# Forty tile transposes of a decoder-block kernel moved from TensorE to DMA on SyncE's queue

## The reference

```
h   = rms_norm(x, norm_mix)
b_a, c_a, u_a, u_p, q_x, g_a, g_p, g_x = split(h @ w_in)                  # 8 x 1024 columns
y_a = (b_a * causal_dwconv3(c_a * u_a)) @ w_conv_out
y_p = per-group linear map of (trailing mean over 2/4/8/16 - token) * pool_scale
y_x = softmax(q_x k^T / 16) v @ w_xattn_out                                # k, v from rms_norm(mem), 256 tokens, 4 heads
x   = x + (sigmoid(g_a)*y_a + sigmoid(g_p)*y_p + sigmoid(g_x)*y_x) @ w_out
h   = rms_norm(x, norm_ffn)
x   = x + (silu(h @ w_gate) * (h @ w_up)) @ w_down                         # 2816 wide
out = rms_norm(x, norm_final)
```

## Time and profile before

| | |
|---|---|
| median of three runs | 1171.29 us |
| the profiled execution | 1170.21 us |
| its span on the slowest core (core 3) | 1168.6 us (all cores 1164.9 to 1168.6) |
| granted TensorE clock, mean | 0.996 to 0.997 |
| TensorE matmul busy | 1137.1 us (97%) |
| VectorE busy | 477.6 us (41%) |
| ScalarE busy | 330.6 us (28%) |
| chain that ended last | PE 91%, DVE 3%, ACT 2%, issue 2%, DMA 1% |
| DMA queue of GpSimd (weights), of SyncE | 39.4%, 14.7% of 16 engines' span |

### The profile page before, as it was taken

One profiled execution on the slowest core, in us unless ns is written; L12 is line 12 of the kernel. 1 busy time (PEld: TensorE's weight loads), 2 busy tenths in 40 slices (PEclk: granted clock), 3 DMA queues, 4 the chain that ended last, 5 costly groups with the idle time before them and its releaser, 6 DMA issues.

```text
span 1168.6 us, 15156 instructions; the slowest of 8 cores (1164.9 to 1168.6 us)
## 1 busy us (share of the span) xinstructions
PE 1137.1 (97%) x5852; PEld 557.7 (48%) x5852; DVE 477.6 (41%) x480; ACT 330.6 (28%) x512; POOL 74.3 (6%) x144
## 2 busy tenths in 40 slices
PE   4899989999999999999999999999999999999997
PEld 2566555454554444444444444444444444444443
DVE  4533555465656654553454632111324221112222
ACT  5333444425222434442121210111524121111111
POOL 1101000101001010001001000200000000000000
PEclk9899999999999999999999999999999999999999
DMA  9999830367296758125226452999954254200132
GB/s 238 174 185 208 140 70 21 80 143 132 62 189 160 223 117 186 38 45 109 49 61 108 64 153 108 177 194 168 191 122 159 90 111 82 43 1 1 36 117 100
DMA packets 35382, 135.89 MB, mean 116 GB/s; under 512 B 4187, under 2 KB 4187, under 8 KB 34800
## 3 DMA queue, kind: packets, MB, share of 16 engines
q0 software_dynamic: 20160, 77.64, 39.4%
q1 hardware_dynamic: 15008, 57.03, 14.7%
q10 hardware_dynamic: 144, 0.26, 0.1%
HBM read 185.27 MB, written 23.07 MB: 178 GB/s over the span
## 4 chain that ended last, share of the span: by engine, by line
PE 91%; DVE 3%; ACT 2%; issue 2%; DMA 1%; DVEq 0%; ACTq 0%; SPq 0%; another core or an unknown queue 0%; POOLq 0%
PE ps L228 89%; PE ps L341 2%; DVE tmp L378 1%; DMA ring<-w_in 1%; ACT tmp L402 1%; DVE tmp L371 1%; ACT tmp L375 0%; DMA arena<-x 0%; DVE smx L399 0%; ACT hb L317 0%; DVE hb L329 0%; DVE arena L383 0%; DVE hA L345 0%; ACT L402 0%; DVE ring L542 0%
## 5 line engine op out<-in xcount | busy, mean ns | idle before, releaser
L228 PE MATMUL ps<-hA,ring 128*128 128x512 bf16 (+1 forms) x2496 | 511.6, 365 | 13.2 <-DVE stat L325 4.5
L228 PEld LDWEIGHTS ps<-hA,ring 128*128 128x128 bf16 x2496 | 244.2, 98 | 271.6 <-issue 16.2
L228 PE MATMUL ps<-arena,ring 128*128 128x512 bf16 (+1 forms) x1600 | 331.4, 366 | 0.1
L228 PEld LDWEIGHTS ps<-arena,ring 128*128 128x128 bf16 x1600 | 156.0, 98 | 167.9 <-issue 0.8
L228 PE MATMUL ps<-arena 128*128 128x512 bf16 x832 | 182.2, 379 | 0.0
L612 DVE TENSOR_TENSOR arena<-ps,tmp 128x1024 bf16<-128x1024 f32 x44 | 53.9, 1224 | 228.5 <-PE ps L228 220.4
L228 PEld LDWEIGHTS ps<-arena 128*128 128x128 bf16 x832 | 80.9, 98 | 95.3
L608 ACT ACTIVATE tmp<-ps 128x1024 f32<-128x1024 f32 x44 | 45.1, 1024 | 253.8 <-PE ps L228 253.8
L453 DVE TENSOR_TENSOR tmp<-tmp 128x1024 f32<-128x1024 f32 (+6 forms) x40 | 49.2, 1230 | 43.0 <-ACT tmp L443 40.5
L228 PE MATMUL ps<-ring,arena 128*128 128x512 bf16 x256 | 57.9, 379 | 0.0
L218 POOL DMA_DIRECT2D ring<-w_in x48 | 25.6, 539 | 445.0 <-PE ps L228 264.3
(11 more groups left out here) (83 smaller groups left out, 614.9 us busy)
## 6 DMA issues: line engine op xcount, KB each, us to landing
ring<-w_in POOLq DMA_DIRECT2D x48, 512.0 KB, 13.7
ring<-w_gate_up POOLq DMA_DIRECT2D x44, 512.0 KB, 14.4
arena<-x SPq DMA_DIRECT2D x32, 512.0 KB, 10.0
tmp<-x_scr SPq DMA_DIRECT2D x24, 512.0 KB, 6.1
x_scr<-arena SPq DMA_DIRECT2D x16, 512.0 KB, 2.9
out<-tmp SPq DMA_DIRECT2D x15, 512.0 KB, 2.9
arena<-w_down POOLq DMA_DIRECT2D x2, 2816.0 KB, 50.1
ring<-w_kv POOLq DMA_DIRECT2D x8, 512.0 KB, 18.4
```

The costliest lines, as they stand in the source:

```text
L228: ins = e.matmul(o, l, r, start=s0, stop=s1)
```

## The change: forty calls of `transpose` become `dma_transpose`

A new helper issues one DMA transpose on SyncE's queue from the `hb` buffer straight to the transposed tile in SBUF. No TensorE instruction, no PSUM bank and no copy remain of these tiles. Two pieces of order change too: the softmax tile's transpose is issued at once after the tile is normalized (the delay of up to two tiles is gone), and `b_trans` follows each `b_fin` at position 1 of a merge chunk instead of position 2.

```diff
+    def dma_transpose(b, dst, dkeys):
+        src = hbt(b)
+        plan.op("sp", lambda e: e.dma_start_transpose(out=dst, in_=src[:, :]), reads=[b.key()], writes=dkeys, dma=True)
...
     def score_t(hf, hbi, i):
-        transpose(hbi, V_PT[hf][0][:, :, i * P:(i + 1) * P], V_PT[hf][1])
+        dma_transpose(hbi, V_PT[hf][0][:, :, i * P:(i + 1) * P], V_PT[hf][1])
...
     def c_trans(b, i, on_dve=False):
-        transpose(b, HA[:, :, TOK0 + i * P:TOK0 + (i + 1) * P], [("HA", i + 1)], on_dve=on_dve)
+        dma_transpose(b, HA[:, :, TOK0 + i * P:TOK0 + (i + 1) * P], [("HA", i + 1)])
...
     def b_trans(i):
-        transpose(b_c[i][0], HB[:, :, i * P:(i + 1) * P], kA(A_H, 8), on_dve=(i % 2 == 0))
+        dma_transpose(b_c[i][0], HB[:, :, i * P:(i + 1) * P], kA(A_H, 8))
...
                 b_fin(i)
+                b_trans(i)
                 b_fin(i + 1)
-        if pos == 2 and j in (2, 3, 5, 6):
-            i = {2: 0, 3: 2, 5: 4, 6: 6}[j]
-            b_trans(i)
-            b_trans(i + 1)
+                b_trans(i + 1)
+        if pos == 2:
             if j == 6:
...
     def s_step(H, i):
-        if len(s_pend) > 1:
-            score_t(*s_pend.pop(0))
-        s_pend.append((H.hf, score(H, i).finish(), i))
+        score_t(H.hf, score(H, i).finish(), i)
```

## The result

The changed kernel takes 1156.19 us (median of five runs; 1155.57 to 1157.67 but for one of 1272.15). The kernel before took 1170.97 us in the same five rounds. The ratio is 0.9873 with a 95% interval of 0.9861 to 0.9886: 14.8 us faster, where the forecast of 1153.5 us meant 17.5 us; the range of 1150 to 1166 holds the time.

A forecast was written before the change was run, and what follows sets the result against it. TensorE, busy 97% of the span, was taken as the bound. 17.8 - 0.45 + 0.57 - 0.5 = 17.4 us off 1170.2 gave 1152.8, on the median's scale 1153.9; forecast 1153.5 us, range 1150 to 1157, about 0.8 for 1150 to 1166.

The forecast's parts named there:

- The block price, 0.445 us, and 40 of them: Each tile's eight transposes cost TensorE 0.445 us; removing 40 such blocks in five stages gains 17.8 us.
- -0.45 and -0.5 in half 0's score stage: One removed block there only lengthens a wait for ScalarE's copy (0.45 us); 0.5 us more kept as a small loss.
- +0.57 for waits for a tile to be transposed: TensorE's waits of 0.40 us at 379.70 and 0.17 us at 428.05 would go too.
- A block that goes is a block gained: Four of five stages have little or no TensorE idle time, so each removed transpose block, 0.445 us, shortens the time.
- the loss of spacing: One-bank transposes spaced the larger products; eviction takes about 1.2 us against 3.45 us of product, so nothing was counted.
- the score stages swallow the gain: Rival, chance 0.12: in half 0 TensorE merely waits longer, all 3.6 us of that stage lost, giving 1157.1 us.
- the 3 us that I had named as a sign of being wrong: The prediction is wrong if new waits on VectorE and ScalarE sum to more than 3 us.
- the 1150 to 1157 given to the forecast: Forecast case, chance 0.64: all half 0 score-stage idle time gone at one end, 3 us lost again at the other.
- T of about 4 us: Time from issue to landing of one 256 KB DMA transpose on SyncE's queue, estimated as twice the store's 2.1 us.
- The upper bound of 11.7 us: Issue-to-landing time if a transpose is cut into 1024 pieces of 256 bytes, 64 per engine, at 183 ns each.
- Up to T = 8.4 us all forty are hidden.: No VO product or FFN of half 1 waits for DMA transposes landing within 8.4 us each; loss from 9.4 us.
- Late weights: Rival, chance 0.06: transposes fill the DMA engines from 372 to 430; weights stall TensorE 9 us, about 1162.5 us.

The follow-up runs named there:

- the deferral in half 1: The changed kernel with the softmax tile's reciprocal, normalization and transpose put behind the next score tile in half 1 only: 1151.24 us.
- the kernel before with the deferred finish: The kernel before, all transposes on TensorE, with each softmax tile's finish put behind the next score tile: 1166.45 us.
- the doubled kernel: The changed kernel with each DMA transpose issued twice in a row, rewriting the same values: 1213.0 us.

## Why the prediction was nearly right, and what it missed

- *The block price, 0.445 us, and 40 of them.* Right. Eight blocks of the down tiles gave 3.58 us, the 24 norm tiles alone 10.2 to 11.7 us for 10.7, and 26 blocks with 1.09 us of waits that went, less 0.33 and 2.05 us of waits that came, make 10.28 us of the measured 10.54.
- *-0.45 and -0.5 in half 0's score stage.* Right in size: the waits there grew from 0.33, 1.95 and 1.83 to 0.89, 1.91 and 1.62 us on core 0, and the five blocks (2.22 us) brought 1.79. I had allowed 0.95 us of loss; 0.43 came.
- *+0.57 for waits for a tile to be transposed.* Right (0.40 and 0.17 us gone); 0.52 us more went at L542 and 0.32 to 0.33 + 0.17 us came at "issue".
- *"A block that goes is a block gained" from 430 to 520.* This step failed. I took the absence of TensorE gaps and the busy shares of VectorE and ScalarE for slack, and set the loss of spacing there to nothing. The chain VectorE, exponentials, VectorE needs 17.6 (before) to 17.85 us per j against the 18.16 that TensorE took. It had 0.3 to 0.5 us to spare per j, 1.96 us in all at the conv_out product, and 0.89 per j, 3.1 in all, was taken away. The price was 2.05 us and, unforeseen, 1.55 us of lower clock: the 3.6 us (3.9 by starts) that the deferral in half 1 gives back. My rival "the score stages swallow the gain" was looking at half 0, where waits already showed, and gave up only 0.12 to it; the swallowing happened in half 1. The new waits on VectorE and ScalarE come to 2.8 us on core 1, just under the 3 us that I had named as a sign of being wrong; the lower clock comes on top. That the time lies 0.8 us inside the 1150 to 1157 given to the forecast is in part luck: the 3 us of loss in that range were meant for half 0's score stage.
- *T of about 4 us.* Right as a median (3.5 and 4.6). The upper bound of 11.7 us rested on a price of 183 ns per packet, and that is refuted. The queue q1 has 57248 - 15008 = 42240 more packets, 1056 per transpose, and the share of 20.9% of 1154.0 us against 14.7% of 1168.6 us makes (0.209 x 1154.0 - 0.147 x 1168.6) x 16 / 42240 = 26 ns each: short packets are cheap. By the Trainium skill, "VectorE: DVE Perf Modes", section "The three transpose paths", eight blocks at 1309 ns would be 10.5 us, an estimate from the page's figure for one; the trace, with 3.5 and 4.6 us for eight blocks in one issue, does not agree.
- *"Up to T = 8.4 us all forty are hidden."* It made no difference here, since nothing waits for a DMA from `hb`, but the working is wrong: it treats T as one number. Two transposes in a row, by medians 6 to 9 us, lost 57 us where the working gives next to nothing, and three lost 177. The long landings read here came where the DMA share was about 1.0, and the transposes, x loads and stores that stood behind them on SyncE's queue were late with them. The margin of the change is smaller than I wrote.
- *Late weights.* The place I named, the products after 442, shows no wait though the DMA share rose to 0.94. What came late were weights in the FFN of half 0, on two cores, 2 us at most, behind the 2816 KB loads of w_down. Before, no core waited more than 0.56 us there, though the same load took 62.1 us on core 1, against 63.5 after. That the transposes' traffic causes the difference is not shown, since the kernel before with the deferred finish has 1.62 us on core 1.

By these terms core 0 comes to 17.8 - 0.43 + 1.09 - 0.50 - 3.60 = 14.4 us; measured are 14.6.

## What to carry to other kernels

Before taking work from an engine that is the bottleneck, add up the period of the other engines' in-order chain in each stage, with the waits inside it: an engine that is busy half of the time can still have only 0.3 to 0.5 us of slack in 18. When the gain falls short, look where the former bottleneck first waits, and move the reader of a slow result one step later on its queue: here that order was worth 4.1 us on the kernel before and 10.5 us on the changed one. A DMA's median time to landing says little of the few that are issued into a burst of large loads; test the margin by issuing it twice, and check what else the second issue holds up, such as its source buffer.

## What the runs showed of the hardware

- A 128x1024 bf16 transpose by DMA, SBUF to SBUF, landed 3.0 us after its issue at the least, 3.1 to 5.1 us by the medians of the kernels here, and 6.3 for `hA<-hb` where a store stood behind each transpose. The one issued at 110.4 us on core 0 took 32.1 us: the DMA share of the ten us from 115 was 1.07, of the ten from 125 1.09.
- It is 1056 packets, of 248 bytes on the mean (67.52 - 57.03 = 10.49 MB more in 42240 packets), at about 26 ns; the second set in the doubled kernel gives (0.252 x 1211.4 - 0.209 x 1154.0) x 16 / 42240 = 24 ns.
- TensorE's granted clock fell to 0.50 behind the wait of 2.05 us at conv_out of half 1, but stayed at 1.00 behind waits of 1.91 us at 146.7 (core 0), 2.02 us at 794.9 (core 1) and 1.35 us at the same conv_out product in the kernel with only the softmax tiles. The length of the wait alone does not decide it; what does stays open.
